# A fused decoder layer on one core: the expert biases added once per block, in two groups of four matmuls on row quarters of the array

## What is computed

```python
def clamped_swiglu(hid):
    x_glu = jnp.minimum(hid[..., ::2], SWIGLU_LIMIT)
    x_lin = jnp.clip(hid[..., 1::2], -SWIGLU_LIMIT, SWIGLU_LIMIT)
    return x_glu * jax.nn.sigmoid(SWIGLU_ALPHA * x_glu) * (x_lin + 1.0)

def expert_block(args):           # for each block of token rows and its expert e
    xb, e = args
    hid = xb @ w1[e] + b1[e]      # w1[e] is 1024 x 2048, b1[e] has 2048 entries
    return clamped_swiglu(hid) @ w2[e] + b2[e]
```

## Time and profile before

| | |
|---|---|
| median of 3 runs (lowest to highest) | 1646.26 us (1645.65 to 1648.67) |
| the profiled execution | 1652.45 us, span 1650.6 us |
| mean granted TensorE clock over the span | 0.959 |
| busy, share of the span: TensorE, VectorE, ScalarE, GpSimd | 95%, 78%, 60%, 9% |
| shares of the chain of waits: TensorE at L1118, at L1143, at L1127 | 42%, 22%, 2% |
| first and last matmul of `add_b1` | 426.9 and 1560.6 us |

### The profile page before, as it was taken

How to read it: one execution, slowest core, us unless ns; L and a number is a source line. 1 busy time by engine, 2 the same in 40 slices (tenths; PEclk the granted TensorE clock), 3 DMA queues, 4 the chain that set the end, 5 groups by cost and what they waited for, 6 DMA issues and landing times.

```text
span 1650.6 us, 20381 instructions
## 1 busy us (share of the span) xinstructions
PE 1573.1 (95%) x6973; PEld 1078.9 (65%) x6973; DVE 1287.8 (78%) x1063; ACT 995.6 (60%) x888; POOL 145.0 (9%) x116
## 2 busy tenths in 40 slices
PE   5999899986899999999999999999999999999987
PEld 3887655553566666666666666666666666666656
DVE  3423233238699999999999999999999999999885
ACT  5423222133477777777777777777777777777632
POOL 5000000002620000000000000000000000000030
PEclk9999688897899999999999999999999999999979
DMA  4128300043799999999999999999999999999951
GB/s 158 51 102 289 138 14 1 13 154 105 261 372 384 366 372 379 374 377 368 367 363 381 377 376 374 368 362 373 374 384 373 370 368 369 372 372 380 374 201 51
DMA packets 130687, 479.00 MB, mean 290 GB/s; under 512 B 9187, under 2 KB 9734, under 8 KB 130662
## 3 DMA queue, kind: packets, MB, share of 16 engines
q1 hardware_dynamic: 119222, 440.24, 71.9%
q0 software_dynamic: 6112, 21.52, 4.1%
q10 hardware_dynamic: 5328, 16.91, 2.7%
HBM read 453.21 MB, written 25.43 MB: 290 GB/s over the span
## 4 chain that ended last, share of the span: by engine, by line
PE 89%; DVE 5%; issue 2%; ACT 2%; DMA 1%; POOL 0%; ACTq 0%; SPq 0%; POOLq 0%; DVEq 0%
PE ps L1118 42%; PE ps L1143 22%; PE ps L949 8%; PE ps L964 4%; PE ps L1127 2%; PE ps L1009 1%; PE ps L1106 1%; PE ps L1150 1%; DVE HL L1480 1%; PE ps L1086 1%; PE ps L1031 1%; PE ps L1217 1%; PE ps L983 1%; DVE H L1555 1%; PE ps L903 1%
## 5 line engine op out<-in xcount | busy, mean ns | idle before, releaser
L1480 DVE TENSOR_TENSOR HL<-W,HL 128x2048 fp32r<-128x2048 f32 x384 | 876.0, 2296 | 75.1 <-ACT HL L741 67.6
L741 ACT ACTIVATE HL<-W 128x2048 fp32r<-128x2048 f32 x384 | 734.9, 1915 | 222.8 <-PE ps L1118 123.5
L1118 PE MATMUL ps<-HL,XTh 128*96 128x512 f32 x2048 | 566.4, 398 | 8.1 <-DVE XTl L1476 4.9
L1118 PEld LDWEIGHTS ps<-HL,XTh 128*96 128x96 f32 x2048 | 324.9, 163 | 141.1 <-issue 5.4
L1118 PE MATMUL ps<-HL,XTl 128*96 128x512 f32 x1024 | 321.2, 395 | 0.0
L1143 PE MATMUL ps<-HL,HIDTh 128*96 128x512 f32 x1024 | 285.9, 401 | 2.6 <-DVE HIDTl L1505 2.6
L1143 PEld LDWEIGHTS ps<-HL,HIDTh 128*96 128x96 f32 x1024 | 160.7, 162 | 83.6 <-issue 15.0
L1118 PEld LDWEIGHTS ps<-HL,XTl 128*96 128x96 f32 x1024 | 165.8, 162 | 71.8 <-issue 0.5
L1143 PE MATMUL ps<-HL,HIDTl 128*96 128x512 f32 x512 | 160.8, 396 | 0.0
L551 POOL DMA_INDIRECT XG<-f_rows,tokix x33 | 64.8, 1963 | 999.6 <-PE ps L1106 998.1
L1143 PEld LDWEIGHTS ps<-HL,HIDTl 128*96 128x96 f32 x512 | 82.8, 162 | 36.0
(11 more groups left out here) (256 smaller groups left out, 1454.6 us busy)
## 6 DMA issues: line engine op xcount, KB each, us to landing
W<-in_w_dram SPq DMA_DIRECT2D x384, 1024.0 KB, 8.3
wst<-in_w_in_dram SPq DMA_DIRECT2D x6, 2048.0 KB, 8.0
y_rows<-actT ACTq DMA_DIRECT2D x32, 384.0 KB, 6.1
y_rows<-M SPq DMA_DIRECT2D x1, 8448.0 KB, 41.9
H<-in_x_dram SPq DMA_DIRECT2D x8, 512.0 KB, 6.4
wst<-in_w_out_dram SPq DMA_DIRECT2D x2, 2048.0 KB, 16.8
W<-in_w_ple_gate_dram SPq DMA_DIRECT2D x4, 1024.0 KB, 8.1
f_rows<-M ACTq DMA_DIRECT2D x4, 512.0 KB, 2.9
```

Of the source, the lines that this page charges most:

```text
L741: act.activation(HL[:, k % HRING, 0], w_slot(k), ACT.Copy).then_inc(w_hi, 1)
L1118: last = pe.matmul(ps[0:CAP, 2 * h + n], xt[:, c], HL[:, s, part, cc * 1024 + n * 512:cc * 1024 + (n + 1) * 512], start=(c == 0 and xt is ...
L1480: dve.tensor_tensor(HL[:, k % HRING, 1], w_slot(k), HL[:, k % HRING, 0].bitcast(F32), ALU.subtract).then_inc(w_lo, 1)
```

## The change

The layout of `BB` becomes: group r of 32 partitions holds the biases of hidden columns 512r to 512r + 511, upper halves in its columns 0 to 511 and remainders in columns 512 to 1023. `add_b1` is called once per block, behind chunk 3, and issues eight matmuls of 32 rows: the upper halves for banks 2, 3, 0, 1, then the remainders for the same banks. Banks 0 and 1 are closed by it; banks 2 and 3 are opened by it, so it also waits for `htl_out`, the w1 matmuls of half 1 no longer open them, and chunk 9 closes them. `clamp(b, 0)` waits for the new count `b1_done`, `clamp(b, 1)` and `split_x(b)` for the use of chunk 9, `choose_bias(b)` for `b1_done` of the block before. The loads, the rounding and the remainder of the biases take the new layout.

```diff
-        b1raw = actT[:].rearrange("p c n -> p (c n)")[:, 0:D]
+        b1raw = actT[:].rearrange("p c n -> p (c n)")[:, 0:512]
...
-        BB_PARTS = 2
+        BB_PARTS = 1
...
-            b1_v = b1[0].rearrange("e (h q n) -> e h q n", h=2, q=2)
             for r in range(4):
-                act.dma_start(b1raw[r * NE:(r + 1) * NE, :].rearrange("e (h n) -> e h n", h=2), b1_v[:, :, r // 2, :]).then_inc(bias_in, 16)
+                act.dma_start(b1raw[r * NE:(r + 1) * NE, :], b1[0, :, r * 512:(r + 1) * 512]).then_inc(bias_in, 16)
...
-            act.activation(BB[:], b1raw, ACT.Copy).then_inc(bb_hi, 1)
+            act.activation(BB[:, 0:512], b1raw, ACT.Copy).then_inc(bb_hi, 1)
...
                 if not first_block(b):
-                    act.wait_ge(h1_done, b * 2)
+                    act.wait_ge(piece_used, chunks(b - 1, 9))
                 act.activation(halves(XTh[:]), ps[:, 6:8, 0:4 * CAP], ACT.Copy).then_inc(xh_ready, 1)
...
-                    act.wait_ge(h1_done, b * 2)
+                    act.wait_ge(b1_done, b)
                 act.activation(sel[:], pair[:, bass.ds(b, 1)].to_broadcast([P, CAP]), ACT.Copy).then_inc(sel_ready, 1)
...
-                                             start=(c == 0 and xt is XTh and part == 0), stop=False)
+                                             start=(h == 0 and c == 0 and xt is XTh and part == 0),
+                                             stop=(h == 1 and c == NC - 1 and xt is XTl))
                 last.then_inc(piece_used, 1)
 
-            def add_b1(b, h):
-                if h == 0:
-                    pe.wait_ge(sel_ready, b + 1)
-                for n in range(2):
-                    rows = slice(n * 2 * NE, (n + 1) * 2 * NE)
-                    last = pe.matmul(ps[0:CAP, 2 * h + n], sel[rows, :], BB[rows, h * 512:(h + 1) * 512], start=False, stop=True)
-                last.then_inc(h1_done, 1)
+            def add_b1(b):
+
+                pe.wait_ge(sel_ready, b + 1)
+                if not first_block(b):
+                    pe.wait_ge(htl_out, b * 2)
+                for part in range(2):
+                    for r in (2, 3, 0, 1):
+                        rows = slice(r * NE, (r + 1) * NE)
+                        last = pe.matmul(ps[0:CAP, r], sel[rows, :], BB[rows, part * 512:(part + 1) * 512], start=(r >= 2 and part == 0),
+                                         stop=(r < 2 and part == 1))
+                last.then_inc(b1_done, 1)
...
                 w1_chunk(b, 3)
-                add_b1(b, 0)
+                add_b1(b)
...
                 w1_chunk(b, 9)
-                add_b1(b, 1)
                 w2_chunk(b, 0, 0, 10, chunks(b, 10))
...
-                dve.wait_ge(h1_done, b * 2 + (h + 1))
+                if h == 0:
+                    dve.wait_ge(b1_done, b + 1)
+                else:
+                    dve.wait_ge(piece_used, chunks(b, 9))
...
-            for r in (1, 3):
-                rows = slice(r * NE, (r + 1) * NE)
-                dve.tensor_tensor(BB[rows, :], b1raw[rows, :], BB[rows, :].bitcast(F32), ALU.subtract).then_inc(bb_ready, 1)
+            dve.tensor_tensor(BB[:, 512:D], b1raw, BB[:, 0:512].bitcast(F32), ALU.subtract).then_inc(bb_ready, 1)
```

More of the change, by code:

```diff
@@ L318, in hybrid_layer @@
         piece_used = sem("piece_used")
-        h1_done = sem("h1_done")
+        b1_done = sem("b1_done")
         moe_step = sem("moe_step")
```

## The result

| | before | after |
|---|---|---|
| median of 4 runs, same session (lowest to highest) | 1647.47 us (1645.65 to 1648.71) | 1635.59 us (1632.29 to 1637.55) |
| the profiled execution, its span | 1652.45, 1650.6 | 1632.29, 1630.4 |
| `add_b1` matmuls, their shapes | 128 of 64 rows | 256 of 32 rows |
| from the first site of block 1 to that of block 31, 30 passes | 466.02 to 1543.02: 35.90 each | 457.67 to 1522.69: 35.50 each |

The ratio is 0.9915, with a 95% interval of 0.9887 to 0.9942: 11.9 us less, where 13.7 had been forecast (1632.6 against 1635.59 measured), well inside the range of 1629 to 1643. Three more timings of the same kernel gave 0.9941 (0.9921 to 0.9961), 0.9909 (0.9891 to 0.9927) and 0.9922 (0.9888 to 0.9955).

A forecast was written before the change was run, and what follows sets the result against it. TensorE's queue was taken to bound the expert stage. Savings of 11.5 (blocks 1 to 31), 1.8 (preparation of `BB`) and 0.4 (block 0) summed to 13.7 us, from a median of 1646.26 to 1632.6 us, range 1629 to 1643.

The forecast's parts named there:

- A site costs 0.60: Each of a block's two old bias sites: 0.60 us on TensorE's chain, 1.20 per block, only 0.23 of each streaming.
- First group of four at the price of a pair: Merged site: the first four 32-row matmuls cost what a pair of halves costs, 0.60 us with entering and leaving.
- Second group adds one stream, 0.23: Merged site: second group's weights load behind the first, adding 0.23 us; site 0.83, saving 0.37 per block.
- The rule of the Trainium skill: Merged site: the second group would pay an open weight load, 0.16 us per block, leaving a 6.5 us gain, not 11.5.
- rival 1: Merged site: second group not free to follow, 0.09 to 0.28 us more per block, 1635.5 to 1641.5 us; chance 0.15.
- Rival 2: Expert stage: weight transfers set the pace, so little beyond the start's 2 us is gained, 1640 to 1644 us; chance 0.06.
- Rival 3: Merged site: quarters do not overlap; in pairs 1647 us (chance 0.07), one at a time 1676 us (chance 0.05).
- rival 4: The change does not do what it says; instruction order left only the eight matmuls' overlap open; no separate chance given.
- `htl_out` and the clamps: Merged site's earlier wait for the hidden remainder, 4 us to spare, and half 0's clamp, 0.1 to spare: cost nothing.
- The preparation of `BB`: Before block 0: two VectorE subtractions become one, 2.50 to 0.70 us on the chain, saving 1.8 us.
- Block 0: Block 0's own sites: the first's added 0.23 us disappears, the second's removal saves 0.60, counted as 0.4.
- 31 times: Blocks 1 to 31: the saving of 0.37 us per block counts 31 times, 11.5 us.

The follow-up runs named there:

- e3: The changed kernel's quarter layout, but with two sites per block as before, each with 2 + 2 matmuls of 32 rows; 1657.08 us, 1.0051 of the kernel before.
- e4: The changed kernel without the eight bias matmuls, b1 left out of the result; 1612.48 us, 0.9761 of the kernel before.
- e8: The changed kernel with only the first group of four 32-row matmuls, bias remainders left out; 1627.45 us, 0.9875 of the kernel before.
- e2: The changed kernel's one site per block, but with four 64-row matmuls and the old layout and loads; 1636.34 us, 0.9924 of the kernel before.
- e1: The changed kernel with its eight matmuls reordered, each quarter's upper halves then at once its remainders; 1636.25 us, 0.9929 of the kernel before.

## Why the prediction was right

- **The bound.** TensorE's queue, by windows and chain. It held in every variant: what the site gained or lost on the chain came back in the pass.
- **A site costs 0.60.** Confirmed from three sides: e3 against before, e4 (0.80 for the new site), e8 (0.58 for one group).
- **First group of four at the price of a pair.** 0.58 measured by e8, 0.60 taken.
- **Second group adds one stream, 0.23.** 0.23 by e8 and the change, 0.20 by e3 against before. The new site was taken at 0.83 and is 0.81; saved per pass 0.40, taken 0.37.
- **The rule of the Trainium skill** ("TensorE: Matmul & The Clock Gate", Part 3, the mechanism: a load overlaps only where the row group differs) would have left 6.5 us of 11.5. The second four weight loads begin 0.09 us after the first, under the running matmuls of the same quarters, and the second group adds its stream and no more. The rule does not hold here, and rival 1 falls with it. The 0.07 us more per group that I estimated from 3.07 in the same part of the Trainium skill are not there either (0.58 against 0.60).
- **Rival 2, the supply**, is ruled out down to 34.70 per pass (e4). **Rival 3** is ruled out by the four matmuls that begin at once; **rival 4** with it.
- **`htl_out` and the clamps** cost nothing, as said. Through all 30 passes TensorE has no wait for `HIDTl`, and VectorE comes to the first clamp at 813.56, 0.15 us after the site's end at 813.41. The one wait for `HIDTl` in the stage, 3.1 us at 1549.58, stands behind block 31, ahead of the last two chunks; before the change it was 2.6.
- **The preparation of `BB`**: 1.8 taken, 2.0 measured at its own place (12.44 to 10.42), but whether it lasts is open: e2, with the old preparation, reaches the first site of block 1 in 64.0 us from the start of the splits, like the change (64.0 to 64.4). The subtraction takes 0.68; the remainder of x followed closer behind it than before.
- **Block 0**: a gain of 0.4 taken, a loss of 1.0 measured, the one term with the wrong sign. A loss of 1.1 us stands ahead of chunk 8. From the first w1 matmul the chain spent 11.06 us on 36 matmuls instead of 10.33, at a granted clock of 0.77 (403.84 to 415.56 us) instead of 0.82 (413.15 to 424.14), and VectorE's split beside GpSimd took 3.62 instead of 3.25, which made the chain's wait before `swiglu` 1.57 instead of 1.20. Behind that, the second site's 0.56 went away and 0.45 came back on the runs of chunks 8, 9 and of block 1's 0, 1 (7.97 instead of 7.76, 5.80 instead of 5.56). The allowance of 0.5 for GpSimd stands in the prediction but not in its sum; for the clock there is none. By the chain this piece is 53.90 here and 53.86, 53.54 and 54.01 in the other profiles of the change; the 52.94 before come from one execution, and e2's 51.57 shows how far such a piece can differ.
- **31 times** should have been 30. Behind the first site of block 31 TensorE no longer sets the end: in both kernels the chain goes from the last use of w2 chunk 5 through ScalarE's move of y, a split, and a transfer of 7.54 us (7.57 before) to the last two chunks. That stretch is 33.96 before and 34.04 after; what the second site's absence saves in it is lost in the longer wait for `HIDTl` (3.1 instead of 2.6).

Term by term: 30 x 0.40 + 2.0 - 1.0 - 0.1 = 12.9 us by the traces, 11.9 by the medians, 13.7 forecast. The mechanism held, and the passes gave 12.0 us where 11.5 had been taken. The part ahead of block 1 gave 1.1 where 2.2 (1.8 + 0.4) had been taken. The two misses go opposite ways, and that they partly cancel is luck.

## What to carry to other kernels

Matmuls of fewer rows inside a stream of full-height ones had a fixed price of about 1.5 streams per visit here (0.35 us, with 96 columns of weights and 512 moving columns), whether they used quarters or halves; what they save must be counted against that, and work of that kind is gathered into one visit. At one visit, count groups, not matmuls: each further group cost one stream. And read the head of a stage apart from its steady part: here a batch of GpSimd work placed in the one block that VectorE leads cost 7 us, and spread over blocks 5 to 14 it cost nothing that the passes show. And measure a saving at the head where the steady part begins, not at its own place: of 2.2 us forecast ahead of block 1, 1.1 arrived.

## What was not expected of the hardware

- Matmuls of free quarters seem to begin ahead of one that waits for its own quarter (e1, argued and not shown): eight in pairs took the 0.64 us of two groups, not the five streams of an ordered start.
- The gap on leaving differs with the number of groups: the next full-height weight load begins 0.24 or 0.25 us after the last of the site's loads when there is one group (before, e8), and 0.39 us after it with two.
- Whether the small matmuls use 64 or 32 rows makes no difference to entering and leaving (0.60 and 0.58 for one group, 0.82 and 0.81 for two).
- VectorE's split of 128x2048 takes 2.29 us alone and 3.6 to 4.3 beside a GpSimd multiplication of 128x1024, and GpSimd's takes 5.4 us on average beside VectorE's work in block 0 (21.64 for four) but 2.4 at the later places.
